# A fused six-layer model on one core: last pairs of the gated recurrences, weight splits, and bias rows of the neighbourhood attention in reversed token order

## The reference, cut to what matters

```python
def _hgrn2_mixer(h, w_in, g_norm, w_out, lb):        # 8 heads of 128
    q, zf, zb, i, g = jnp.split(h @ w_in, 5, axis=-1)
    ...  # forget gates from zf (forward) and zb (backward), keys = 1 - gate
    def per_seq(a):
        fwd = _gla_chunk_scan(q_s, kf_s, v_s, lf_s)
        bwd = _gla_chunk_scan(q_s[:, ::-1], kb_s[:, ::-1], v_s[:, ::-1], lbw_s[:, ::-1])[:, ::-1]
        return fwd + bwd
    o = _rms_norm(o, g_norm) * jax.nn.silu(gh)
    return o.reshape(B, T, D_MODEL).astype(h.dtype) @ w_out

def _na_mixer(h, w_in, q_norm, k_norm, rpb, w_out):  # 16 heads of 64, a grid of 4 rows of 64
    q, k, v = jnp.split(h @ w_in, 3, axis=-1)        # q, k then normed per head
    ...
        s = jnp.einsum('bqhd,brkhd->bhqrk', q_r, k_blk).astype(jnp.float32) * scale
        s = jnp.where(col_mask[:, None, :], s + bias, NEG_INF)   # bias from rpb, by row and column offset
        p = jax.nn.softmax(s.reshape(B, NA_HEADS, GRID_W, win_r * GRID_W), axis=-1)
        return jnp.einsum('bhqrk,brkhd->bqhd', p, v_blk)
    return o @ w_out
```

## Time and profile before

| | |
|---|---|
| three runs, us | 3058.28, 3063.12, 3063.68 |
| profiled execution, us | 3055.57 |
| its span, us | 3053.80 |
| mean granted PE clock | 0.969 |
| PE busy | 2855.1 us, 93% |
| PEld busy | 2639.7 us, 86% |
| DVE busy | 2002.9 us, 66% |
| ACT busy | 1426.9 us, 47% |
| POOL busy | 98.7 us, 3% |

### The profile page before, as it was taken

How to read it: one execution, slowest core, us unless ns; L and a number is a source line. 1 busy time by engine, 2 the same in 40 slices (tenths; PEclk the granted TensorE clock), 3 DMA queues, 4 the chain that set the end, 5 groups by cost and what they waited for, 6 DMA issues and landing times.

```text
span 3053.8 us, 46734 instructions
## 1 busy us (share of the span) xinstructions
PE 2855.1 (93%) x19701; PEld 2639.7 (86%) x19701; DVE 2002.9 (66%) x2615; ACT 1426.9 (47%) x1904; POOL 98.7 (3%) x148
## 2 busy tenths in 40 slices
PE   7999979999988999999999999997999699896998
PEld 6999869999975999998799999996999599794897
DVE  5667766565657666557665665776656677746777
ACT  4445544444444544445554444554444444453443
POOL 0000000000002000001100000000000100000000
PEclk9999999999999999999999999998999899997999
DMA  7654326675541565553256566432664456442562
GB/s 227 188 161 138 112 82 215 186 207 186 159 145 49 184 184 183 182 167 93 94 181 186 166 200 186 132 125 69 199 185 154 138 173 200 152 156 65 166 192 98
DMA packets 404726, 478.41 MB, mean 157 GB/s; under 512 B 16555, under 2 KB 331653, under 8 KB 404517
## 3 DMA queue, kind: packets, MB, share of 16 engines
q1 hardware_dynamic: 400944, 467.33, 48.8%
q0 software_dynamic: 1776, 6.77, 0.8%
q10 hardware_dynamic: 1796, 1.33, 0.1%
HBM read 474.32 MB, written 1.05 MB: 156 GB/s over the span
## 4 chain that ended last, share of the span: by engine, by line
PE 82%; DVE 10%; ACT 4%; issue 3%; ACTq 0%; DVEq 0%
PE Wk L621 17%; PE Wk L623 16%; PE Wk L622 16%; PE Y L621 9%; PE Y L622 9%; PE Y L623 9%; DVE w_lo L1747 2%; DVE work L1986 1%; ACT w_hi L1246 1%; PE Y L971 1%; PE Y L874 1%; PE Y L726 1%; PE Wk L944 1%; PE Wk L960 0%; PE Wk L874 0%
## 5 line engine op out<-in xcount | busy, mean ns | idle before, releaser
L1747 DVE TENSOR_TENSOR w_lo<-ring,w_hi 128x1024 fp32r<-128x1024 f32 (+2 forms) x910 | 1070.4, 1200 | 690.1 <-ACT w_hi L1246 643.7
L621 PE MATMUL Wk<-xT_hi,w_hi 128*128 128x256 f32 x4320 | 1233.3, 285 | 21.0 <-DVE xT_lo L1786 17.7
L623 PE MATMUL Wk<-xT_hi,w_lo 128*128 128x256 f32 x4320 | 1225.6, 284 | 0.0
L622 PE MATMUL Wk<-xT_lo,w_hi 128*128 128x256 f32 x4320 | 1225.6, 284 | 0.0
L1246 ACT ACTIVATE w_hi<-ring 128x1024 fp32r<-128x1024 f32 (+1 forms) x894 | 906.8, 1039 | 645.0 <-PE Wk L623 431.7
L621 PEld LDWEIGHTS Wk<-xT_hi,w_hi 128*128 128x128 f32 x4320 | 832.2, 193 | 28.2 <-issue 14.8
L622 PEld LDWEIGHTS Wk<-xT_lo,w_hi 128*128 128x128 f32 x4320 | 832.4, 193 | 4.7 <-issue 0.9
L623 PEld LDWEIGHTS Wk<-xT_hi,w_lo 128*128 128x128 f32 x4320 | 831.9, 193 | 0.0
L621 PE MATMUL Y<-w_hi,hid_hi 128*128 128x512 f32 x904 | 353.5, 391 | 4.3 <-DVE hid_lo L1840 4.3
L622 PE MATMUL Y<-w_lo,hid_hi 128*128 128x512 f32 x904 | 352.1, 389 | 0.0
L623 PE MATMUL Y<-w_hi,hid_lo 128*128 128x512 f32 x904 | 350.9, 388 | 0.0
(11 more groups left out here) (283 smaller groups left out, 2829.1 us busy)
## 6 DMA issues: line engine op xcount, KB each, us to landing
ring<-in_ffn_w_gu SPq DMA_DIRECT2D x352, 512.0 KB, 4.4
ring<-in_ffn_w_down SPq DMA_DIRECT2D x224, 512.0 KB, 4.4
ring<-in_ffn_w_up SPq DMA_DIRECT2D x96, 512.0 KB, 5.9
ring<-in_hg_w_in SPq DMA_DIRECT2D x80, 512.0 KB, 3.6
ring<-in_na_w_in SPq DMA_DIRECT2D x24, 512.0 KB, 4.5
ring<-in_hg_w_out SPq DMA_DIRECT2D x16, 512.0 KB, 3.6
ring<-in_lru_w_in SPq DMA_DIRECT2D x16, 512.0 KB, 4.4
ring<-in_kv_w SPq DMA_DIRECT2D x16, 512.0 KB, 4.5
```

The source lines that it names most:

```text
L621: pe.matmul(o, l_hi, r_hi, start=first, stop=False)
L622: pe.matmul(o, l_hi, r_lo, start=False, stop=False)
L623: return pe.matmul(o, l_lo, r_hi, start=False, stop=last)
L1747: ins = dve.tensor_tensor(l, r, h.bitcast(F32), ALU.subtract)
```

## The change

In the recurrences:

1. In pairs 0 to 2 (the first three), `ahead` moves up within a round, ahead of the reading of z and q on DVE and ahead of the sigmoid's steps, the squares, the roots and the reading of values on ACT.
2. The first two pairs' results are split into hid_hi and hid_lo instead of xT, the first one a pair earlier (round 5 of pair 2), the second in round 0 of the last pair; that of pair 2 in round 5.
3. In the last pair PE computes half 0 of tile 0 behind round 0, half 0 of tile 1 behind round 2, half 1 of tile 0 behind round 4 and half 1 of tile 1 behind round 6. The weight order of these four halves is changed to match. The output projection's first halves no longer wait for pair 2's result.
4. The mean of squares of pair 2 goes to bank 0 and waits for the queries of the last pair to be read.
5. In the last pair the splits follow a table, HALVES_LAST. Behind round 8, `ahead` goes on to the third half tile of the next layer on both engines; DVE's `splits` behind the recurrence goes away.

In the neighbourhood attention: the bias rows are loaded in the other order of rows and stay mirrored, the mask is mirrored, queries are written backwards within each 128 tokens (two rows of 64), and the result of each column is written backwards again. `flip`, its copies and their waits go, and with them the matrix in the constants. POOL's bias additions wait for the DMA and the first normed unit.

"The latent attention" in the change's name stands in both versions alike; the shared helper gets one more dimension there of size one.

```diff
-MS_BANKS = (4, 4, 4, 2)
+MS_BANKS = (4, 4, 0, 2)
+HALVES_LAST = (0, 0, 1, 1, 2, 2, 3, 4, 5)
...
+        if subs[s][0] == "hg":
+            order[-8:-4] = [(t1 - 4, 0), (t1 - 3, 0), (t1 - 4, 1), (t1 - 3, 1)]
...
+        def backwards(a):
+            return a.rearrange("p k (tt t) -> p (k tt) t", t=P)[:, :, ::-1]
...
-                    src = bass.AP(rpb.tensor, rpb.offset + (4 - h) * NA_COLS + 15 - (GRID_W - 1),
+                    src = bass.AP(rpb.tensor, rpb.offset + (3 + h) * NA_COLS + 15 - (GRID_W - 1),
...
-                    pool.wait_ge(na_flipped, NA_H // 2)
+                    pool.wait_ge(na_in, 32)
+                    pool.wait_ge(p_out, units_before(s) + 1)
...
-                    if p_ + 1 < HG_PAIRS:
+                    if p_ + 2 < HG_PAIRS:
                         pe.wait_ge(g_saved, Q + 2)
+                    elif p_ + 1 < HG_PAIRS:
+                        pe.wait_ge(q_saved, Q + 2)
                     pe.matmul(bank(MS_BANKS[p_]), ones, hg_sq[:, 0, :], start=True, stop=True).then_inc(ms_psum, 1)
...
-                    if j == 0 and n == 0:
-                        pe.wait_ge(g_saved, Q0 + HG_PAIRS)
-                        pe.wait_ge(o_ready, Q0 + HG_PAIRS - 1)
-                    y_half(out_of(base[s] + 5 * HG_PAIRS, j), n, first=j == 0)
+                    if j == 0:
+                        pe.wait_ge(*((o_ready, Q0 + HG_PAIRS - 1) if n else (g_saved, Q0 + HG_PAIRS)))
+                    t = base[s] + 5 * HG_PAIRS
+                    a = (t + j, pair_of(hid_hi, j), pair_of(hid_lo, j)) if j < 2 else out_of(t, j)
+                    y_half(a, n, first=j == 0)
...
-                        if last and 3 <= i < 7:
-                            pair_out((i - 3) // 2, (i - 3) % 2)
+                        if last and i in (0, 2, 4, 6):
+                            pair_out(i // 2 % 2, i // 4)
...
-                def flip(r):
-                    if r >= 2:
-                        pe.wait_ge(na_flipped, r - 1)
-                    pe.matmul(bank(4 + r % 2)[:, 0:2 * NA_RUN], cst[:, Const.FLIP:Const.END],
-                              na_R[:, 2 * r:2 * r + 2, :].rearrange("p h n -> p (h n)"), start=True, stop=True)\
-                        .then_inc(na_flips, 1)
...
-                    flip(i - 1)
-                pe.wait_ge(na_flipped, NA_H // 2)
...
+            def ahead(n, s, over=False):
+                while nxt[0] <= nth[split_units_of(s)[0]] + n and (over or split_units[nxt[0]][0] < end[s]):
...
+                        if last and i == 1:
+                            squares_of(p_ - 1)
...
+                        if not last:
+                            ahead(HALVES_AHEAD + 10 * (p_ + 1) + i, s)
...
-                        ahead(HALVES_AHEAD + 10 * (p_ + 1) + i, s)
+                        else:
+                            ahead(HALVES_AHEAD + 38 + HALVES_LAST[i], s)
+                ahead(10 * HG_PAIRS + 10, s, over=True)
...
+                elif src.shape[1] != n:
+                    hi, lo = backwards(hi), backwards(lo)
...
+                    if pp >= 2:
+                        split_out(2 * pp, 2, hg_o[:, pp, :], (o_high, Q0 + pp + 1), o_split)
+                        return
+                    dve.tensor_copy(hid_hi[:, pp, :], hg_o[:, pp, :]).then_inc(o_high, 1)
+                    dve.wait_ge(o_high, Q0 + pp + 1)
+                    dve.tensor_tensor(hid_lo[:, pp, :], hg_o[:, pp, :], hid_hi[:, pp, :].bitcast(F32), ALU.subtract)\
+                        .then_inc(o_split, 1)
...
-                        if last and i in (1, 2):
-                            split_pair(i - 1)
+                        if p_ == HG_PAIRS - 2 and i == 5:
+                            split_pair(0)
+                        if last and i in (0, 5):
+                            split_pair(1 + i // 5)
                         if p_ and i == 6 - 3 * last:
                             normed(p_ - 1)
-                            if last:
-                                split_pair(2)
                         if not last:
+                            ahead(HALVES_AHEAD + 10 * (p_ + 1) + i, s)
...
-                        ahead(HALVES_AHEAD + 10 * (p_ + 1) + i, s)
+                        else:
+                            ahead(HALVES_AHEAD + 38 + HALVES_LAST[i], s)
+                ahead(10 * HG_PAIRS + 10, s, over=True)
...
-                    dve.wait_ge(na_flips, i + 1)
-                    dve.tensor_copy(na_R[:, 2 * i:2 * i + 2, :].rearrange("p h n -> p (h n)"),
-                                    bank(4 + i % 2)[:, 0:2 * NA_RUN]).then_inc(na_flipped, 1)
...
-                    o = (na_q if i < 4 else na_k)[:, 2 * (i % 4):2 * (i % 4) + 2, :].rearrange("p a b -> p (a b)")
-                    dve.scalar_tensor_tensor(o, bank(S_BANKS[i % 3]), na_gain[:, i // 4:i // 4 + 1], na_rs[:, u % 2, :],
-                                             ALU.mult, ALU.mult).then_inc(p_out, 1)
-                dve.wait_ge(na_flipped, NA_H // 2)
+                    o = (na_q if i < 4 else na_k)[:, 2 * (i % 4):2 * (i % 4) + 2, :]
+                    o = backwards(o) if i < 4 else o.rearrange("p k (tt t) -> p (k tt) t", t=P)
+                    z, rs = (a.rearrange("p (a t) -> p a t", t=P) for a in (bank(S_BANKS[i % 3]), na_rs[:, u % 2, :]))
+                    dve.scalar_tensor_tensor(o, z, na_gain[:, i // 4:i // 4 + 1], rs, ALU.mult, ALU.mult)\
+                        .then_inc(p_out, 1)
...
-                splits(end[s] + 1)
+                if kind != "hg":
+                    splits(end[s] + 1)
...
-    f[:, Const.COLS:Const.CAUSAL] = np.tile(np.where(inside, 0, -1e30), (2, 1))
+    f[:, Const.COLS:Const.CAUSAL] = np.tile(np.where(inside[::-1], 0, -1e30), (2, 1))
```

More of the change, by code:

```diff
@@ L1454, in hgrn @@
                             g_sigmoid(Q)
-                        if p_ and i == 3 - 2 * last:
+                        if not last:
+                            ahead(HALVES_AHEAD + 10 * (p_ + 1) + i, s)
+                        if p_ and i == 3 and not last:
                             squares_of(p_ - 1)
@@ L1754, in splits, with ahead @@
                     nxt[0] += 1
-            def ahead(n, s):
-                while nxt[0] <= nth[split_units_of(s)[0]] + n and split_units[nxt[0]][0] < end[s]:
+            def ahead(n, s, over=False):
+                while nxt[0] <= nth[split_units_of(s)[0]] + n and (over or split_units[nxt[0]][0] < end[s]):
                     low(split_units[nxt[0]])
@@ L2070, in attention @@
                         g = h // per
[L2071 removed]
+                        o = bank(4 + g % 2)[:, 0:T].rearrange("p (a t) -> p a t", a=split)
+                        split_out(g, 1, o, (s_high, g0 + g + 1), s_saved)
             def softmax_probs(h, H, at_p):
@@ L2125, in na @@
                 splits(base[s] + 14)
-                attention(s, NA_H, scores, lambda h, H: softmax_probs(h, H, na_p), 2)
+                attention(s, NA_H, scores, lambda h, H: softmax_probs(h, H, na_p), 2, split=TT)
             def mla(s):
```

18 lines of the change are left out of this document (7 added, 11 removed).

## The result

| | before | after |
|---|---|---|
| median of the runs, us | 3063.4 (3058.3 to 3063.8, 4 runs) | 3008.16 (3007.2 to 3010.0, 4 runs) |
| ratio | | 0.9824, interval 0.9807 to 0.9841 |
| profiled execution, its span, us | 3055.57, 3053.8 | 3007.2, 3005.4 |
| granted clock, mean | 0.969 | 0.975 |

The kernel is 55 us faster by the medians and 48.4 us by the two profiles. The forecast was 3012, from a saving of 50.6.

What follows compares the result with a forecast made beforehand. TensorE (PE), 82% of the chain, was taken as the bound. Per recurrence 11.4 + 11.7 - 2.0 - 2.0 = 19.1; two give 38.2, plus 12.4 makes 50.6 us off the 3063.12 median: 3012 us, range 2996 to 3038.

Steps and rivals of the forecast that it cites:

- Part 1: Neighbourhood attention: without eight turning products and the stop behind them, 12.4 us saved, bounds 10.5 and 13.
- Backward writes: Attention's queries and results written backwards on DVE: 0 us taken, bounds 0 and 3; 8.4 us if at twice the duration.
- Part 2: First three pairs of each recurrence: weight splits earlier in a round save 11.4 us a recurrence, bounds 5 and 14.
- left-over waits: PE's waits expected to remain per recurrence: 4.5 us in the first three pairs, 12.0 us in the last pair.
- Part 3: Last pair of each recurrence: output projection halves placed between scores save 11.7 us, bounds 6 and 17.
- Part 4: End of each recurrence: fourth w_lo falls behind DVE's wait for r_row, 2.0 us lost, bounds 1 and 3.
- The clock: Last pair's remaining stops cost clock: 2 us charged a recurrence, bounds 0 and 6.
- rival C: Slower: PE falls to 1.2 GHz in the recurrences and stays; at 0.75 clock 37 us a recurrence, 3086 us; chance 0.05.
- A: First three pairs: splits were free anyway, gain about 2 instead of 11.4 us a recurrence, 3031 us; chance 0.17.
- B: Last pair then waits on the chain score, doubling, split, score: gains only 6 us, total 3024 us; chance 0.14.
- D: Only the attention's saving works, the recurrences' changes cancel: 3051 us; chance 0.06.

## Why the prediction was right, step by step

- **Part 1, the attention, 12.4 us.** 12.9 between the marks and 13.5 in the run of this part alone. The value product came 11.3 us earlier (10.9 said), and the rest behind it, the clock above all, gave 1.6 (1.5 said). The run with the products kept puts 7.1 us on the stop and the clock behind it, where the sum had 4.10 and 1.5 and the passes next to the stop. Backward writes at 0: the three durations are the same to the nanosecond or two, so neither the bound of 3 us nor the 8.4 us of the other end was needed.
- **Part 2, the first three pairs, 11.4 us a recurrence.** The profile gives 134.29 - 122.56 = 11.7; the run alone 26.5 for two. The left-over waits were 0.73, 1.50, 0.55 and 0.72 us (3.5 against 4.5), and the clock rose to 1.00 as the sum assumed. That the total fits so well is partly luck: the waits gave 10.7 - 3.5 = 7.2 us instead of 6.2, the clock the other 4.5 instead of 5.2, and by pair the left-over waits were 2.2, 0.6 and 0.7 where 1.7, 1.0 and 1.8 were forecast. One reason in this step was wrong: the prediction put w_lo's place on DVE beside w_hi's place on ACT as a cause. ACT's alone gives all of it (30.0 us), and DVE's costs 2.0 to 2.5 us a recurrence by the two pairs of traces.
- **Part 3, the last pair, 11.7 us.** 10.7 in the first recurrence of the profile and 10.3 in the second. These hold what the clock costs, so they stand against 11.7 - 2.0 = 9.7. Of the seven left-over waits, third score 1.6 was 1.41, fifth 2.8 was 2.54, the half behind it 1.3 was 1.02, seventh 1.7 was 1.45, ninth 2.1 was 1.60, copy ahead of the output 1.0 was 0.69, last normalisation 1.5 was 1.38. Each was a little shorter (10.1 against 12.0), and the wait ahead of the transposes fell from 2.13 to 0.35. The work was priced too low: in the stretch below PE is busy 35.9 us and not 33.2, of which the clock at 0.96 makes 0.04 x 46 = 1.8 us (charged apart in the sum) and work under its price the other 0.9. Waits priced 1.9 us too high and work priced too low cancel for the most part; that is luck, too.

```profile
370.00:416.00 46.00, 35.92 (x176) 29.04 (x176) 31.99 (x48) 20.46 (x30) 0.00 (x0) 0.96 0.33 103
```

- **Part 4, the loss of 2.0 us.** The wait for w_lo is 1.73 us and the marks step by 2.0, in both recurrences. The fourth half split ahead takes it away.
- **The clock, 2 us a recurrence.** A range rather than a number. Two profiles of the changed kernel have the same waits in the last pair to within 0.02 us, and yet it takes 46.2 us in one and 418.89 - 369.56 = 49.3 in the other. The same four microseconds of the first and the second profile, behind the stops of 2.54 and 1.02 us:

```profile
390.00:394.00 4.00, 3.57 (x17) 2.82 (x16) 1.81 (x4) 0.46 (x1) 0.00 (x0) 0.85 0.27 72
```

```profile
390.00:394.00 4.00, 4.00 (x12) 3.13 (x12) 1.33 (x3) 0.36 (x1) 0.00 (x0) 0.50 0.28 85
```

  0.50 of full speed is the lower of the two levels, 1.2 GHz. In the second profile PE went at it for the whole of these four microseconds. The rule of the Trainium skill that the prediction cited ("TensorE: Matmul & The Clock Gate", Why this matters for your kernels) is borne out so far as the clock fell behind stops, to 0.50 here. The clock was back at 0.96 to 1.00 from 394 to 402 us in both, so rival C (PE stays at 1.2 GHz) didn't happen. The second profile shows one more fall, 0.82 and 0.83 from 402 to 412 us, behind the stops of 1.62 and 0.69 us. The last pair of the second recurrence took 46.50 and 46.49 us in these two profiles, so only one of the four last pairs took 3 us more.
- **The rivals.** A is out by the runs of the pairs alone. B, the chain score, doubling, copy, score, is what the left-over waits are, but at 10.7 instead of 6 us of gain. C was priced too low: 148 us of work at a mean clock of 0.75 take 49 us longer, not 37, and a loss of 25 us goes with 0.86, not 0.83; nothing hung on it. D is out, since the recurrences carry three quarters of the gain.
- **The forecast of 3012 us.** 3008.16 were measured. The saving was 50.6 us by the sum, 48.4 by the profiles and 55.2 by the medians. The sum was built on the profile of before, 7.8 us under the median, and subtracted from the median; the errors of the parts are smaller than the 7 us between these two ways of measuring, so the closeness of 3012 to 3008 says less than the waits and stretches above.

## What to carry to other kernels

What follows is this kernel's experience, not tried on another. An instruction that only feeds a buffer (here the weight copy) should stand in its queue ahead of one that waits for another engine, and not behind it. It is enough to move it on the engine that makes the other one idle: on the second engine it is better to do first the work whose input is already there. When one engine alternates with another in a chain, put independent matmuls right behind the step whose answer takes longest, and look for idle time already paid for (DVE ahead of the residual) when a small piece of work needs a place.

## What the runs showed of the hardware that was not expected

- VectorE wrote float32 and its rounded form to addresses that run backwards at the same speed as forwards: 409 to 426 ns for the two writes of 128x256, 750 to 752 ns for 128x512, both directions within these limits.
- The granted clock behind the same stops differs between executions of one program: 0.85 in one and 0.50 in another over the same 4 us. All of it together was worth 3.1 us in the last pair. In the 14 us behind the first recurrence of before's instructions it was 1.00 in one execution and 0.89 in two others, 1.4 to 1.6 us. So a single profile resolves a recurrence to about 3 us, however exact its waits are.
- Stops of 0.55 to 1.5 us in the first three pairs left the clock at 1.00 there. In the last pair the stop ahead of the ninth score (1.60 and 1.62 us) had a fall to 0.82 and 0.83 behind it in one profile and none in the other, where the clock stayed at 1.00. The length of the last stop alone doesn't decide it.
